# Other byte offsets for the moving tokens and silu products of five feed-forward blocks, and another kind of waiting turn

## The reference

```
def swiglu(h, w_gate, w_up, w_down):
    return (jax.nn.silu(h @ w_gate) * (h @ w_up)) @ w_down

# first stack: layer 0 = even_mixer + swiglu (hidden width 2816)
#              layer 1 = gated_deltanet + moe_swiglu (8 experts, 2 chosen for each token, hidden width 3584)
# second stack, for l in 0, 1:
#   x = x + 0.5 * swiglu(rms_norm(x), ...)      (hidden width 2816)
#   x = x + mixer(rms_norm(x)) @ w_out[l]
#   x = x + 0.5 * swiglu(rms_norm(x), ...)      (hidden width 2816)
```

## The kernel before

| tile | start | start modulo 128 |
|---|---|---|
| mix_parts (shares its place with mslot0 to 2) | 16512 | 0 |
| small, and in it the column of w_a (2880 further) | 82080 | 32 |
| mslot3_parts | 101952 | 64 |
| scratch, weights_hi0 to 2, weights_lo0 to 2 (8192 each) | 134720 | 64 |
| x_parts | 183872 | 64 |
| hidden_hi, hidden_lo (2048 each) | 200256 | 64 |
| mixer_lows | 204352 | 64 |
| x_pair | 212544 | 64 |

## Time and profile before

### The profile page before, as it was taken

How to read it: one execution, slowest core, us unless ns; L and a number is a source line. 1 busy time by engine, 2 the same in 40 slices (tenths; PEclk the granted TensorE clock), 3 DMA queues, 4 the chain that set the end, 5 groups by cost and what they waited for, 6 DMA issues and landing times.

```text
span 2399.3 us, 34175 instructions
## 1 busy us (share of the span) xinstructions
PE 2377.6 (99%) x12542; PEld 2017.8 (84%) x12542; DVE 1873.0 (78%) x1961; ACT 1437.8 (60%) x1474; POOL 14.3 (1%) x34
## 2 busy tenths in 40 slices
PE   8999999999999999999999999999999999999998
PEld 7788899888888888888888888888788888897887
DVE  7767786678888888888889898677966676788666
ACT  6645455467777777777777776455254454544444
POOL 1000000000000000000000010000000000000000
PEclk9999999999999999999999999999999999999999
DMA  8375243459999999999999997753355666533653
GB/s 302 114 254 176 69 137 137 150 208 372 382 379 349 377 379 382 349 376 381 381 349 375 380 395 252 267 178 121 132 193 183 196 227 231 175 119 123 202 190 125
DMA packets 315952, 603.73 MB, mean 252 GB/s; under 512 B 9120, under 2 KB 135200, under 8 KB 315552
## 3 DMA queue, kind: packets, MB, share of 16 engines
q1 hardware_dynamic: 314160, 592.70, 69.6%
q10 hardware_dynamic: 1136, 7.87, 0.8%
q0 software_dynamic: 576, 2.10, 0.2%
HBM read 597.91 MB, written 8.91 MB: 253 GB/s over the span
## 4 chain that ended last, share of the span: by engine, by line
PE 94%; DVE 3%; ACT 1%; DMA 1%; DVEq 1%; issue 0%; SPq 0%; ACTq 0%
PE bank L205 20%; PE bank L207 19%; PE bank L206 19%; PE bank L1218 17%; PE bank L1222 8%; PE bank L3513 1%; PE bank L2955 1%; PE bank L3440 1%; PE bank L2230 1%; PE bank L2240 1%; DMA mslot<-in_e_w_in 1%; PE bank L2930 1%; PE bank L1714 1%; PE bank L1058 0%; PE bank L2149 0%; PE bank L2249 0%
## 5 line engine op out<-in xcount | busy, mean ns | idle before, releaser
L3205 DVE TENSOR_TENSOR weights_lo<-mslot,weights_hi 128x2048 fp32r<-128x2048 f32 x336 | 767.5, 2291 | 112.5 <-ACT weights_hi L3098 111.8
L3098 ACT ACTIVATE weights_hi<-mslot 128x2048 fp32r<-128x2048 f32 x336 | 644.2, 1920 | 212.5 <-PE bank L207 209.8
L1370 DVE TENSOR_TENSOR weights_lo<-scratch,weights_hi 128x2048 fp32r<-128x2048 f32 x165 | 377.4, 2290 | 165.8 <-ACT weights_hi L1363 165.7
L1218 PE MATMUL bank<-x_parts,weights_hi 128*128 128x512 f32 x1760 | 441.2, 392 | 1.8 <-DVE x_parts L921 1.8
L1218 PEld LDWEIGHTS bank<-x_parts,weights_hi 128*128 128x128 f32 x1760 | 319.5, 189 | 63.7 <-DVE x_parts L921 2.4
L205 PE MATMUL bank<-weights_hi,x_pair 128*128 128x512 f32 x896 | 354.2, 395 | 0.2 <-issue 0.2
L207 PE MATMUL bank<-weights_hi,x_pair 128*128 128x512 f32 x896 | 349.3, 390 | 0.0
L206 PE MATMUL bank<-weights_lo,x_pair 128*128 128x512 f32 x896 | 349.1, 390 | 0.0
L1363 ACT ACTIVATE weights_hi<-scratch 128x2048 fp32r<-128x2048 f32 x165 | 314.6, 1909 | 49.9 <-PE bank L207 48.9
L205 PE MATMUL bank<-weights_hi,hidden_hi 128*128 128x512 f32 x808 | 315.9, 391 | 0.0
L206 PE MATMUL bank<-weights_lo,hidden_hi 128*128 128x512 f32 x808 | 315.0, 390 | 0.0
(11 more groups left out here) (561 smaller groups left out, 2737.4 us busy)
## 6 DMA issues: line engine op xcount, KB each, us to landing
mslot<-in_o_moe_w_gate SPq DMA_DIRECT2D x112, 1024.0 KB, 6.5
mslot<-in_o_moe_w_up SPq DMA_DIRECT2D x112, 1024.0 KB, 6.9
mslot<-in_o_moe_w_down SPq DMA_DIRECT2D x112, 1024.0 KB, 6.8
scratch<-in_ffn_w_gate SPq DMA_DIRECT2D x44, 1024.0 KB, 5.4
scratch<-in_ffn_w_up SPq DMA_DIRECT2D x44, 1024.0 KB, 5.4
scratch<-in_ffn_w_down SPq DMA_DIRECT2D x44, 1024.0 KB, 5.2
mslot<-in_o_w_in SPq DMA_DIRECT2D x7, 2048.0 KB, 11.1
scratch<-in_e_ffn_w_gate SPq DMA_DIRECT2D x11, 1024.0 KB, 5.4
```

Of the source, the lines that this page charges most:

```text
L1218: pe.matmul(m.ps[bank + j][:, :], hi[:, k, cols(j)], both, start=(k == 0), stop=False)
L1370: dve.tensor_tensor(m.wlo[to][:, :], m.fslot[i], m.whi[to][:, :], ALU.subtract).then_inc(m.sig["f_lo"], 1)
L3098: act.activation(m.whi[(place + half) % PLACES][:, :], r.slot[slot + half], ACT.Copy).then_inc(s["r_hi"], 1)
L3205: dve.tensor_tensor(m.wlo[i][:, :], r.slot[slot + half], m.whi[i][:, :], ALU.subtract).then_inc(s["r_lo"], 1)
```

## The change

Three things are done:

- The tokens' parts of block v start `AT_BLOCK[v]` elements of 4 bytes further inside `x_parts`, which is made 192 bytes longer: 64, 192, 32, 16 and 160 bytes for v = 0 to 4. So do the silu products' parts.
- `hidden_lo` has no tile of its own any more: it lies in the columns of the parameters w_a and w_i inside `small`, at byte 85056 (64 modulo 128) and `AT_BLOCK[v]` further. These parameters are read in the first mixer only. `hidden_hi` is 192 bytes longer, and starts 192 bytes later, since `x_parts` is longer. `mixer_lows` and `x_pair` keep their places.
- The 14 transposes behind the experts become 20 products of type `float32r`, 14 of them with 96 and 6 with 192 moving columns.

The distance of the products, in bytes modulo 128:

| products | before | after, for v = 0, 1, 2, 3, 4 |
|---|---|---|
| wide and narrow | 0 | 64, 64, 32, 16, 32 |
| down, stationary hidden_hi | 0 | 0, 0, 32, 48, 32 |
| down, stationary hidden_lo | 0 | 64, 64, 96, 112, 96 |
| down of the last step, stationary x_parts | 0 | 64, 64, 96, 112, 96 |
| experts' down, stationary hidden_hi | 0 | 64 |
| experts' down, stationary hidden_lo | 0 | 0 |
| experts' gate and up, and their last down | 0 | 0 |

The diff, without the lines in which only a name is replaced:

```diff
+AT_BLOCK = (16, 48, 8, 4, 40)
+SPARE = max(AT_BLOCK)
+HL_AT = 24
...
+    with nc.sbuf_tensor("small_parts", [P, SMALL_W], F32R) as small_parts:
+        at = SMALL_COLS["w_a"][0] + HL_AT
+        m.hl = small_parts[:, at:at + HALF + SPARE]
     small = sb("small", SMALL_W)
...
-    m.x2 = cut(sb("x_parts", KT * 2 * SEQ, F32R), 0, KT, 2, SEQ)
+    x_parts = sb("x_parts", KT * 2 * SEQ + SPARE, F32R)
+    m.x2 = cut(x_parts, 0, KT, 2, SEQ)
+    m.x2_of = [cut(x_parts, at, KT, 2, SEQ) for at in AT_BLOCK]
     m.xh, m.xl = m.x2[:, :, 0, :], m.x2[:, :, 1, :]
-    m.hh, m.hl = sb("hidden_hi", HALF, F32R), sb("hidden_lo", HALF, F32R)
...
+    m.hh = sb("hidden_hi", HALF + SPARE, F32R)
+    free = f0 - 6 * PIECE - KT * 2 * SEQ - HALF - 2 * SPARE
+    with nc.sbuf_tensor("mixer_lows", [P, free + 16 + 3 * PIECE], F32R) as lows:
+        m.c_low = [cut(lows, free + 16 + i * KT * DC, KT, DC) for i in range(2)]
+    sb("scratch_rest", free + PIECE)
...
-            both = m.x2[:, k].rearrange("p i t -> p (i t)")
+            both = m.x2_of[v][:, k].rearrange("p i t -> p (i t)")
...
-                last = pe.matmul(m.ps[bank + j][:, 0:SEQ], lo[:, k, cols(j)], m.xh[:, k, :],
+                last = pe.matmul(m.ps[bank + j][:, 0:SEQ], lo[:, k, cols(j)], m.x2_of[v][:, k, 0, :],
...
-def ffn_hidden(m, last):
+def ffn_hidden(m, v, last):
+    at = AT_BLOCK[v]
     if last:
-        x2 = m.x2.rearrange("p k i t -> p (k i t)")
+        x2 = m.x2_of[v].rearrange("p k i t -> p (k i t)")
         pair = [x2[:, i * HALF:(i + 1) * HALF] for i in (6, 7)]
     else:
-        pair = [m.hh[:, :], m.hl[:, :]]
+        pair = [m.hh[:, at:at + HALF], m.hl[:, at:at + HALF]]
...
+def keep_busy_parts(pe, m, widths):
+    for n in widths:
+        pe.matmul(m.ps[0][:, 0:n], m.hh[:, 0:P], m.hh[:, 0:n], start=True, stop=True)
...
-    keep_busy(pe, m, 14)
+    keep_busy_parts(pe, m, 8 * (96,) + 6 * (192, 96))
```

More of the change, by code:

```diff
@@ L186, in place @@
     m.wlo = [sb(f"weights_lo{i}", PIECE, F32R) for i in range(3)]
-    m.x2 = cut(sb("x_parts", KT * 2 * SEQ, F32R), 0, KT, 2, SEQ)
+    x_parts = sb("x_parts", KT * 2 * SEQ + SPARE, F32R)
+    m.x2 = cut(x_parts, 0, KT, 2, SEQ)
+    m.x2_of = [cut(x_parts, at, KT, 2, SEQ) for at in AT_BLOCK]
     m.xh, m.xl = m.x2[:, :, 0, :], m.x2[:, :, 1, :]
-    m.hh, m.hl = sb("hidden_hi", HALF, F32R), sb("hidden_lo", HALF, F32R)
-    with nc.sbuf_tensor("mixer_lows", [P, 16 + 3 * PIECE], F32R) as lows:
-        m.c_low = [cut(lows, 16 + i * KT * DC, KT, DC) for i in range(2)]
-    sb("scratch_rest", PIECE)
+    m.hh = sb("hidden_hi", HALF + SPARE, F32R)
[3 more added lines that the diff above has]
+    sb("scratch_rest", free + PIECE)
     m.xg = cut(sb("x_pair", 2 * PIECE, F32R), 0, 2, KT, 2 * P)
@@ L920, in ffn_entry_low @@
         dve.wait_ge(s["n_xh"], KT // 2 * m.splits[u] + k // 2 + 1)
-        dve.scalar_tensor_tensor(m.xl[:, k, :], turned(m, u, k),
-                                 gain[:, k:k + 1], m.xh[:, k, :], ALU.mult, ALU.subtract).then_inc(s["n_xl"], 1)
+        both = m.x2_of[m.splits[u]]
+        dve.scalar_tensor_tensor(both[:, k, 1, :], turned(m, u, k),
+                                 gain[:, k:k + 1], both[:, k, 0, :], ALU.mult, ALU.subtract).then_inc(s["n_xl"], 1)
 def ffn_entry_dve(dve, m, u, gain, v, scale):
@@ L1015, in tokens @@
             act.wait_ge(s["n_tr"], rows_turned(m, u) + k // 2 + 1)
-            last = act.activation(m.xh[:, k, :], turned(m, u, k), ACT.Copy, scale=gain[:, k:k + 1])
+            last = act.activation(m.x2_of[m.splits[u]][:, k, 0, :], turned(m, u, k), ACT.Copy, scale=gain[:, k:k + 1])
             if k % 2 == 1:
@@ L1271, in down_part @@
         hi, lo = parts(ffn_place(v, "down", NU - 1 if final else None), D)
-        hh, hl = ffn_hidden(m, last=final)
+        hh, hl = ffn_hidden(m, v, last=final)
         cols, tok = slice(half * HALF, (half + 1) * HALF), slice(t * P, (t + 1) * P)
@@ L1455, in hidden @@
     def hidden(u, last=False):
-        hh, hl = (flat(t) for t in ffn_hidden(m, last))
+        hh, hl = (flat(t) for t in ffn_hidden(m, v, last))
         for j, cols in enumerate(halves):
@@ L2797, in moe_mem @@
     r.oh32, r.ohT = r.oh.bitcast(F32), m.ohT.rearrange("p (e t) -> p e t", e=2)
-    r.hh, r.hl = (t[:, :].rearrange("p (j t) -> p j t", j=FC // P) for t in (m.hh, m.hl))
+    r.hh, r.hl = (t[:, 0:HALF].rearrange("p (j t) -> p j t", j=FC // P) for t in (m.hh, m.hl))
     r.hh_last, r.hl_last = (x2[:, i * FC:(i + 1) * FC].rearrange("p (j t) -> p j t", j=FC // P) for i in range(2))
```

## The result

The changed kernel takes 2410.25 us (median of 5 runs, 2409.71 to 2411.18) against 2401.59 for the kernel before on the same chip: a ratio of 1.0036, 95% interval 1.0025 to 1.0047. It is 8.7 us slower. The forecast was 2395.5 in a range of 2385 to 2410, so the sign is wrong and the time lies just outside the range. The rival called *Slower* had given 2409.1 us.

A forecast was written before the change was run, and what follows sets the result against it. TensorE was taken as the bound, so all hung on product pitch. Narrow -10.0, wide -0.7, dense downs 0, experts' downs +4.1 and turns +0.4 summed to -6.2 us: 2395.5 us, range 2385 to 2410.

The forecast's parts named there:

- Slower: Rival: operand reads disturb each other more in long products at the new distances; +7.4 us, 2409.1 us; chance 0.20.
- Narrow: Dense blocks' 1760 products of 256 columns: from 119 ns to 113.3, a gain of 10.0 us.
- in the fast rhythm 113.3: Quicker of two pitches seen for 256 columns at distance 64, taken for narrow products; the slow one, 117.8, gains 2.1 us.
- Wide: Dense blocks' 1760 products of 512 columns: from 229.1 ns to about the 228.7 seen at distance 64, -0.7 us.
- 64 is the nearest row for all of them: Narrow products at 64, 16 or 32 bytes were all priced from trace pitches measured at distance 64.
- Dense downs: Dense blocks' 1320 down products, 227.9 ns now: 0 us likeliest, with +3.4 us in the other cases.
- The mixed rows: Earlier trace's short 512-column streams mixing distances 0 and 64: 230.5 and 231.9 ns, +3.4 or +5.3 us for dense downs.
- Experts' downs: Experts' stage: 1224 down products moved to 64 (high) and 0 (low) get slower, +4.1 us.
- Turns: Waiting turns behind the experts: 20 short products replacing 14 transposes cost +0.4 us.
- What costs nothing: ScalarE's and VectorE's writes keep shapes and counts, any slowing hides in slack, and hidden_lo's new place adds no wait.
- The rule weighed in the prediction: TensorE has two independent SBUF read ports, so starts change nothing; its rival: +0.4 us, 2402.1 us, chance 0.12.
- the sign for the sum: All 512-column products: the prediction is wrong in sign if they rise by more than 3.3 ns.

The follow-up runs named there:

- e1_tokens: Kernel before with only the tokens' parts moved, by 64, 192, 32, 16 and 160 bytes in the five blocks; 2403.38 us, ratio 1.0007.
- e7: Kernel before with only low weights of gate and up moved, 64 and 192 bytes in blocks 0 and 3, one by 192 in block 1; 2401.20 us.
- e11: Kernel before with all tokens at distance 64, some narrow products at 192, and hidden_hi unintentionally 64 bytes off; 2408.71 us, ratio 1.0029.
- e13: Same as e11 but with the high silu products back at distance 0; 2399.71 us, ratio 0.9990 to the kernel before.
- e5_all64: Kernel before with only the tokens' parts moved, by 64 bytes in all five blocks; 2399.01 us, ratio 0.9989.
- e2_downs: Kernel before with only the dense blocks' silu products placed as in the change; 2408.08 us, ratio 1.0026.
- e3_experts: Kernel before with only the experts' high silu products moved, to distance 64; 2404.46 us, ratio 1.0012.
- e9_low_silu: Kernel before with only the low silu products moved, by 64 bytes, in dense blocks and experts; 2411.38 us, ratio 1.0037.
- e6: Kernel before with only the tokens' parts moved, by 192, 64, 128, 96 and 224 bytes in the five blocks; 2404.24 us, ratio 1.0010.
- e10: Kernel before with only the tokens' parts moved, by 8, 48, 80, 240 and 112 bytes in the five blocks; 2406.27 us, ratio 1.0018.

## Why the prediction was wrong

The sum was -6.2 us and the trace has +8.8. The 15 us between are in the first three terms, each read from rows of other stages (+5.0, +5.6 and +5.0; the experts' downs give 1.1 back):

- **Narrow, -10.0 forecast, -5.0 measured.** That they get faster at the change's offsets is right (e1_tokens). But their own distance is not the whole of it: changed alone, by the low weights, it took 1.2 and 1.1 ns off them in blocks 0 and 3 (e7), where the moved tokens took off 2.3 to 4.1 at 64 and 192 bytes (e1). The step that failed is "in the fast rhythm 113.3" as the state of all of them; they came to 116.1 outside of waits, from 119.05. The earlier trace rows had shown the same instructions at 117.8 and the prediction took the better of two rhythms. e11 against e13 shows that what stands ahead chooses between them, at the same distance. At 64 bytes in all blocks 59 of 220 sets ran at 113.3, and the mean with all hand-overs and waits is 118.4. The rows themselves were those of another distance, too: modulo 256 they are at 192, where only block 1 came to lie.
- **Wide, -0.7 forecast, +4.9 measured.** The row at 64 bytes was sound for 64 bytes: block 0 stayed at 230.5 and e5_all64 costs 0.4 us in all five. What failed is that this row was taken for all five blocks, as in "64 is the nearest row for all of them", which the prediction says of the narrow ones, and under it the count of distances modulo 128, by which 192 was taken for 64. At 192 the wide products take 233.4, at 16, 32 and 160 bytes 232.8 to 234.8, and no row of 512 columns had these distances. That the bound of +4.9 at 231.9 ns was met is luck: it came from dearer pitches in four blocks and none in the fifth.
- **Dense downs, 0 forecast, +5.0 measured** (e2_downs alone: +4.7). The mixed rows had given +3.4 to +5.3, and they were set aside as short and irregular: "I take 0 in the likeliest case". e2_downs shows that they were right in size. The 0 itself had no row for it.
- **Experts' downs, +4.1 forecast, +3.0 measured** in the change and +3.0 in e3_experts. Right in mechanism and in size, between its bounds of 2.4 and 6.4. That a loss there costs in full held too: the stage is 2.9 us longer. Whether the transfers would shut in a gain was not tested.
- **Turns, +0.4 forecast, +0.55 measured.** Right: the first wide product now waits for them.
- **What costs nothing** did: VectorE and ScalarE are as busy as before, and no wait was added.

The rule weighed in the prediction (the Trainium skill, "TensorE: Matmul & The Clock Gate", What happens when you issue a matmul, step 1: loading the next weights takes no read bandwidth from the running product) would have made the change worth its turns alone, 2402.1 us. The runs do not bear out what was drawn from it for these products: e3_experts puts one operand's start 64 bytes off and pays 2.8 us, and e9_low_silu 9.3. They do not show whether it is the two reads that get in each other's way, so they do not settle the rule itself.

Of the signs that the prediction had named, 0.91 us for narrow sets appeared, and 5.53 us or more for 24 downs appeared only in the dense blocks (5.60; 5.49 in the experts). The sign "if blocks 0 and 1 (distance 64) differ from blocks 2 and 4 (32) and 3 (16)" was too coarse: blocks 0 and 1 differ from each other as well. And the sign for the sum was misplaced: the long products rose by (4.9 + 5.0 + 3.0) / 4304 = 3.0 ns, under the 3.3 of the prediction, and yet the change is slower. 3.3 ns with the fast rhythm is where it would be 4.8 us slower; the gain is used up at (10.0 - 0.4) / 4304 = 2.2 ns already, and with the measured 5.0 in place of 10.0 at 1.1 ns.

What stays open is the mechanism inside the engine. That the reads of the two operands meet in the memory is one way to tell it, and no run here isolates it. Nor did a run move both operands of all products of a kind by the same bytes, so that their difference counts, and not each start by itself, is the simplest reading and not shown. That e2_downs and e1_tokens do not add is shown, but by which path a phase is carried through several hundred products is not.

## What to carry to other kernels

When a stream of products has no wait in it, the start of its moving operand against that of its stationary one is a setting like a tile size: it moved a product by up to 8.4 ns of 227 here (the third ones of e9_low_silu, 227.0 to 235.4), and it must be measured for the very pair of shapes, since long and short products were fastest at different distances (0 or 64 and 192). Moving one tile moves all that lie behind it, so the distance of every pair should be listed, modulo 256 bytes at least, before a layout is changed. And where the trace shows two pitches for one shape, the forecast's term is their mix as the phase gives it, not the better one; an unmeasured setting is to be priced by the nearest rows even if they are few.

## What the runs showed of the hardware

Mean ns from start to start, with the products at each hand-over in it, by the distance in bytes modulo 256 (tokens alone moved, one block each, from e1, e5, e6 and e10; before: 0):

```
distance   0     8    16    32    48    64    80    96   112   128   160   192   224   240
wide    230.5 234.5 232.8 234.4 233.4 230.7 232.2 234.7 231.9 233.5 234.8 233.4 234.0 234.6
narrow  120.5 122.7 118.1 119.0 120.4 118.2 120.3 122.0 119.1 120.1 119.6 116.4 120.1 119.4
```

- The blocks' own means at distance 0 run from 230.0 to 230.9 and from 120.5 to 121.1, so differences under 1 ns say little. No steady stream of 512 columns ran below 226.7 and none of 256 columns below 113.3. The pair is cheapest at 64 (348.9 together, against 351.0 at 0), then at 192 (349.8).
- 24 downs in one steady stream take 226.7 each at distance 0; with the high part at 64 the experts' mean rose from 227.5 to 229.8, with the low part at 192 to 231.5, with the high part at 192 to 233.7.
- Streams without a wait repeat: in the kernel before, the sets of eight narrow products away from waits have means of 118.6 to 119.1 ns in all five blocks.
- The 200 products of 256 columns in the mixer behind block 3 took 118.4 ns or 115.8 with the same instructions and the same places, 0.5 us apart, in runs in which nothing near them differed (118.4 before, 115.8 with the turns alone changed). The difference lies in those of the earlier trace rows: in the 32 such mixers of the 16 traces they take the fast rhythm 20 times and the slow one 12 times. Such a flip is larger than some effects studied here, and only the trace tells it from them.
